# Moving the convolution of a hybrid mixer to VectorE, and reordering the banks, steps and last projections of three mixers

## What is computed

```python
for l in range(2):
    h = rmsnorm(x, norm_mix[l])
    x = x + (even_mixer(h, ...) if l % 2 == 0 else odd_mixer(h, ...))
    x = x + swiglu(rmsnorm(x, norm_ffn[l]), ...)      # d_ff = 2816
```

```python
x = layer_norm(alpha * x + 0.5 * swiglu_2(x, ...))    # d_ff = 4096
x = layer_norm(alpha * x + hybrid_mixer(x, ...))
x = layer_norm(alpha * x + 0.5 * swiglu_2(x, ...))
```

## Time and profile before

| | |
|---|---|
| time, median of 3 runs | 2555.53 us (2553.45 to 2555.55) |
| the profiled execution's own time | 2554.28 us |
| its span, first to last instruction | 2552.2 us |
| PE busy | 2431.1 us, 95% |
| DVE busy | 1801.2 us, 71% |
| ACT busy | 1304.5 us, 51% |
| POOL busy | 115.7 us, 5% |
| mean granted TensorE clock | 0.974 |

### The profile page before, as it was taken

How to read it: one execution, slowest core, us unless ns; L and a number is a source line. 1 busy time by engine, 2 the same in 40 slices (tenths; PEclk the granted TensorE clock), 3 DMA queues, 4 the chain that set the end, 5 groups by cost and what they waited for, 6 DMA issues and landing times.

```text
span 2552.2 us, 39046 instructions
## 1 busy us (share of the span) xinstructions
PE 2431.1 (95%) x15856; PEld 2221.0 (87%) x15856; DVE 1801.2 (71%) x2679; ACT 1304.5 (51%) x1995; POOL 115.7 (5%) x104
## 2 busy tenths in 40 slices
PE   7789999989999999889998999999998899989998
PEld 7678889887888888889998888898888899988887
DVE  4659757567867876777467876688767664678864
ACT  5545454545544544556454554455445663545543
POOL 0002100001200000210000000000002100000000
PEclk9899999999999999999999999999999899999999
DMA  5236565344656565533253656556664332446652
GB/s 182 83 112 213 180 209 181 129 133 144 191 185 198 190 187 185 179 122 108 92 164 126 206 185 187 166 187 198 186 187 160 112 111 97 158 134 204 188 175 91
DMA packets 114882, 409.92 MB, mean 161 GB/s; under 512 B 12816, under 2 KB 14992, under 8 KB 114704
## 3 DMA queue, kind: packets, MB, share of 16 engines
q1 hardware_dynamic: 114704, 407.43, 49.9%
HBM read 406.33 MB, written 1.05 MB: 160 GB/s over the span
## 4 chain that ended last, share of the span: by engine, by line
PE 86%; DVE 9%; ACT 4%; issue 1%; DMA 0%; SPq 0%; ACTq 0%; DVEq 0%
PE ps L359 85%; DVE wlo L1655 3%; ACT whi L1007 1%; ACT region L1170 1%; PE ps L568 0%; DVE x L1812 0%; DVE x L1830 0%; DVE region L1855 0%; DVE xx L1710 0%; DVE region L1950 0%; DMA cst<-in_consts 0%; DVE region L2226 0%; DVE region L2184 0%; DVE region L2312 0%; DVE region L2223 0%
## 5 line engine op out<-in xcount | busy, mean ns | idle before, releaser
L359 PE MATMUL ps<-xx,whi 128*128 128x256 f32 (+1 forms) x4912 | 1346.9, 345 | 40.5 <-ACT region L1404 16.1
L1655 DVE TENSOR_TENSOR wlo<-raw,whi 128x1024 fp32r<-128x1024 f32 (+3 forms) x772 | 935.6, 1217 | 444.5 <-ACT whi L1007 442.9
L1007 ACT ACTIVATE whi<-raw 128x1024 fp32r<-128x1024 f32 (+3 forms) x772 | 800.7, 1043 | 531.4 <-PE ps L359 531.0
L359 PE MATMUL ps<-xx,wlo 128*128 128x256 f32 x3688 | 1046.3, 284 | 0.0
L359 PEld LDWEIGHTS ps<-xx,whi 128*128 128x128 f32 x4912 | 864.8, 193 | 156.5 <-ACT region L1404 16.5
L359 PEld LDWEIGHTS ps<-xx,wlo 128*128 128x128 f32 x3688 | 709.9, 192 | 0.3
L359 PE MATMUL ps<-H,whi 128*128 128x512 f32 (+1 forms) x2400 | 686.7, 351 | 22.1 <-DVE wlo L1655 10.4
L359 PE MATMUL ps<-H,wlo 128*128 128x256 f32 x1888 | 534.7, 283 | 0.0
L359 PEld LDWEIGHTS ps<-H,whi 128*128 128x128 f32 x2400 | 425.5, 191 | 86.4 <-issue 14.6
L359 PEld LDWEIGHTS ps<-H,wlo 128*128 128x128 f32 x1888 | 358.9, 190 | 0.2
L1650 DVE TENSOR_REDUCE t<-ps 128x256 f32<-128x512 f32 x308 | 211.7, 689 | 51.5 <-PE ps L359 42.4
(11 more groups left out here) (271 smaller groups left out, 1564.0 us busy)
## 6 DMA issues: line engine op xcount, KB each, us to landing
raw<-in_sg SPq DMA_DIRECT2D x128, 512.0 KB, 3.8
raw<-in_su SPq DMA_DIRECT2D x128, 512.0 KB, 3.5
raw<-in_sd SPq DMA_DIRECT2D x128, 512.0 KB, 3.9
raw<-in_mw_g SPq DMA_DIRECT2D x48, 512.0 KB, 3.5
raw<-in_fg SPq DMA_DIRECT2D x44, 512.0 KB, 3.4
raw<-in_fu SPq DMA_DIRECT2D x44, 512.0 KB, 3.6
raw<-in_fd SPq DMA_DIRECT2D x32, 512.0 KB, 3.5
raw<-in_mw_a SPq DMA_DIRECT2D x24, 512.0 KB, 3.8
```

Source lines behind the costliest of these rows:

```text
L359: return e.matmul(out, lhsT, rhs, start=start, stop=stop, skip_group_check=True)
L1007: e.activation(m.whi[:, c % NHL, 0:cw], m.raw[:, c % NRAW, 0:cw], ACT.Copy).then_inc(s["whi"].h, s["whi"].up(c))
L1655: e.tensor_tensor(m.wlo[:, c % NHL, 0:cw], m.raw[:, c % NRAW, 0:cw], m.whi[:, c % NHL, 0:cw].bitcast(F32), ALU.subtract).then_inc(s["wlo"] ...
```

## The change

**Projections end two tiles at a time.** The last four chunks of `ew_out` and `ow_out` are laid out anew, so that one chunk holds the last 512 input rows for two output tiles. `gemm_last` runs them: after each chunk one bank is finished. Each of its chunks needs all four of the last input tiles.

**Banks of the feed-forward networks after a rmsnorm.** `first_bank` makes them start at bank 4; the statistics go to bank 3. One weight chunk more is made ahead of the statistics (`produce(1)`).

**even().** Two chunks of `ew_v` come ahead of `ukv`. `k_pe` is made transposed (16 matmuls of 512 and 256 columns), summed by one reduce and transposed back by two transposes; VectorE sums the squares so that four one-column matmuls are left of 20. Two chunks, not four, are made ready before x is split, and ScalarE's first table load is taken by a dummy instruction at the start. One gelu of 128 x 1024 replaces four of 128 x 256. The side steps in the first four `ew_out` chunks are two to a chunk.

**odd().** Heads start at chunks 0, 7 and 14 of `ow_g` and at chunk 4 of `ow_out`, with more empty steps inside; `side.finish()` stands once, ahead of `gemm_last`.

**hybrid().** All convolution taps but the first are made by VectorE; GpSimd keeps the copies of the identity. `mw_c` uses banks 0 to 3, its scaled bias is computed first, two of the six `raw` go behind it, the wait for `rowc` moves back. `attend` has a further empty step in places, `delta()` starts one chunk later. In `mw_o` tiles 0 to 7 use banks 2, 3, 4, 5, 0, 1, 6, 7, the centring uses bank 1, and one `chunk()` moves ahead of `norm_tile(2)`.

```diff
@@ weight_order()
-    o = [("ew_c", i) for i in range(5)] + [("ew_pe", 0)]
+    o = [("ew_c", i) for i in range(5)] + [("ew_pe", 0), ("ew_v", 0), ("ew_v", 1)]
...
+def first_bank(kind, j):
+
+    return 2 * ((j + (2 if kind == "rms" else 0)) % 4)
...
+    m.mo_bank = [2, 3, 4, 5, 0, 1, 6, 7]
@@ tensor_program
+    def gemm_last(name, i, tag, hb):
+
+        for p in range(4):
+            wh, wl = weights(name, i + p)
+            for n in range(2):
+                o = ps[p][:, n * 256:n * 256 + 256]
+                for k in range(4):
+                    w.wait_ge(s["hlo"], *tag(k))
+                    c = (n * 4 + k) * 128
+                    t = mm3(o, wh[:, c:c + 128], wl[:, c:c + 128], hb[0][:, k, :], hb[1][:, k, :], False, k == 3)
+            t.then_inc(s["gemm"].h, s["gemm"].up(name, i + p))
@@ ffn
-            return take(2 * (j % 4) + g, ("fsum", st, j, g))
+            return take(first_bank(kind, j) + g, ("fsum", st, j, g))
...
-            rms_stats(st)
+            rms_stats(st, bank=3)
@@ even, TensorE
-        gemm_tm("ew_pe", 0, [take(5, ("edve", "kpe"))], xh, xl, 8, 8, 32)
-        b = take(6, ("root", "rr", 1))
+        wh, wl = weights("ew_pe", 0)
+        b = take(5, ("edve", "kpf"))
+        for k in range(8):
+            c = slice(k * 32, k * 32 + 32)
+            mm(b[0:32, :], wh[:, c], m.xx[:, k].rearrange("p a b -> p (a b)"), start=k == 0, stop=False)
+            t = mm(b[0:32, 0:256], wl[:, c], xh[:, k, :], start=False, stop=True)
...
+        value(0)
+        w.wait_ge(s["edve"], "kpf")
...
+        value(1)
...
         for k in range(4):
             w.wait_ge(s["hlo"], "ea", k)
-            gemm_acc("ew_out", k, h1[0], h1[1], k, k == 0, False, readers)
-            side.step()
-        for k in range(4):
-            side.until(lambda: k in ot)
-            w.wait_ge(s["hlo"], "eo", k)
-            gemm_acc("ew_out", 4 + k, h2[0], h2[1], k, False, k == 3, readers)
+            gemm_acc("ew_out", k, h1[0], h1[1], k, k == 0, readers, side.step)
             side.step()
         side.finish()
+        gemm_last("ew_out", 4, lambda k: ("eo", k), h2)
@@ odd, TensorE
         for i in range(16):
             gemm_fm("ow_g", i, take(i % 4, ("rdve", "g", i))[:, 0:256], xh, xl)
-            if i in (6, 12):
-                side.add(head(0 if i == 6 else 1))
+            if i in (0, 7, 14):
+                side.add(head(i // 7))
+            side.step()
+        readers = [[("xadd", "f1", p)] for p in range(4)]
+        for c in range(12):
+            h, k = c // 4, c % 4
+            w.wait_ge(s["hlo"], "o", c)
+            gemm_acc("ow_out", c, hb[h % 2][0], hb[h % 2][1], k, c == 0, readers)
+            if c == 4:
+                side.add(head(3))
             side.step()
         side.finish()
...
+        gemm_last("ow_out", 12, lambda k: ("o", 12 + k), h2)
@@ even, ScalarE
-            w.wait_ge(s["edve"], "u", i)
-            e.activation(m.euF[:, i, :], m.euF[:, i, :], ACT.Gelu_apprx_tanh).then_inc(s["eact"].h, s["eact"].up("u", i))
...
+            if i == 3:
+                w.wait_ge(s["edve"], "u", 3)
+                e.activation(m.euF[:, :, :], m.euF[:, :, :], ACT.Gelu_apprx_tanh).then_inc(s["eact"].h, s["eact"].up("u"))
@@ hybrid, VectorE
         def conv(i):
+
             y, pr = m.cv[:, i, :], m.pr[i]
-            w.wait_ge(s["cpool"], l, i)
...
+            w.wait_ge(s["pact"], l, "a3", i)
+            for d in (1, 2, 3):
+                e.scalar_tensor_tensor(y[:, d:256], pr[:, 0:256 - d], pk(f"cw{l}", 12 * (3 - d) + i), y[:, d:256], ALU.mult,
+                                       ALU.add).then_inc(s["cdve"].h, s["cdve"].up(l, d, i))
+                w.wait_ge(s["cdve"], l, d, i)
+
...
         for n in range(8):
-            norm_tile(f"t{l}", (f"l2g{l}", f"l2b{l}"), n, 3, add_one, (f"mw_o{l}", n), n)
-            if n >= 3:
+            if n == 2:
+                chunk()
+            norm_tile(f"t{l}", (f"l2g{l}", f"l2b{l}"), n, 3, add_one, (f"mw_o{l}", n), m.mo_bank[n])
+            if 3 <= n < 7:
                 chunk()
@@ hybrid, GpSimd
-        for i in range(12):
-            pr, y, r = m.pr[i], m.cv[:, i, :], m.tap[i % 2]
-            w.wait_ge(s["pact"], l, "a", i)
-            if i >= 2:
-                w.wait_ge(s["cpool"], l, i - 2)
-            e.tensor_scalar(r, pr, pk(f"cw{l}", 24 + i), None, ALU.mult).then_inc(s["cpool"].h, s["cpool"].up(l, "r", i))
-            w.wait_ge(s["cpool"], l, "r", i)
-            w.wait_ge(s["pact"], l, "a3", i)
-            e.tensor_tensor(y[:, 1:256], y[:, 1:256], r[:, 0:255], ALU.add).then_inc(s["cpool"].h, s["cpool"].up(l, i))
-        w.wait_ge(s["cpool"], l, 11)
+        w.wait_ge(s["gemm"], f"mw_a{l}", 7)
```

More of the change, by code:

```diff
@@ L428, in gemm_tm, with gemm_acc @@
                 after()
-    def gemm_acc(name, i, ah, al, k, first, last, readers):
+    def gemm_acc(name, i, ah, al, k, first, readers, half=None):
         wh, wl = weights(name, i)
@@ L448, in rms_stats @@
             w.wait_ge(s["xsq"], st, 7)
[L449 removed]
+        b = take(bank, ("root", st))
         mm(b[:, 0:256], m.onm, acc[0], start=True, stop=False)
@@ L559, in attend @@
                     yield
-            for _ in range(gap):
+            for _ in range(gaps[h0 // 4]):
                 yield
@@ L645, in even @@
         side.add(heads(1))
-        gemm_tm("ew_v", 0, [take(2 + tt, ("eact", "v", tt)) for tt in range(2)], xh, xl, 8, 2, 512, after=side.step)
+        for c in (2, 3):
+            value(c)
+            side.step()
         for i in range(4):
@@ L1189, in even @@
         rms_parts("e", "nm0", ("in",))
-        chunk(4)
-        chunk(0)
+        chunk(2)
+        chunk()
         rms_stats("e", RT=True)
+        for _ in range(2):
+            chunk()
         for i in range(5):
-            if i == 4:
-                chunk()
             dst = m.cq[:, i, :] if i < 3 else m.ckv[:, i - 3, :]
@@ L1303, in even @@
             side.step()
-        for k in range(4):
-            side.until(lambda: k in ot)
-            chunk()
             side.step()
         side.finish()
+        for _ in range(4):
+            chunk()
     def odd():
@@ L1356, in odd @@
             e.activation(m.sg[:, i, :], m.sg[:, i, :], ACT.Silu).then_inc(s["ract"].h, s["ract"].up("g", i))
-            if i in (6, 12):
-                side.add(head(0 if i == 6 else 1))
+            if i in (0, 7, 14):
+                side.add(head(i // 7))
+            side.step()
+        for c in range(12):
+            chunk()
+            if c == 4:
+                side.add(head(3))
             side.step()
         side.finish()
-        for h in range(4):
-            if h < 3 and h + 1 not in ot:
-                side.add(head(h + 1))
-            for k in range(4):
-                if k == 0 and h not in ot:
-                    side.finish()
-                chunk()
-                side.step()
-            side.finish()
+        for _ in range(4):
+            chunk()
     def hybrid(l):
@@ L1395, in hybrid @@
             tap(i)
-        for i in range(6, 8):
+        for i in range(4):
+            produce(1, 4)
+            raw(i)
+        for _ in range(2):
             chunk()
-            taps(i)
         for i in range(5):
@@ L1454, in hybrid @@
             taps(i)
-            if i == 11:
-                for p in range(5):
-                    conv(p)
             side.step()
@@ L1543, in hybrid @@
                 s["pact"].h, s["pact"].up(l, "qk", i))
-            if i == 1:
-                conv(5)
+            if i == 2:
+                for p in range(6):
+                    conv(p)
                 side.add(delta())
@@ L1598, in hybrid @@
                 w.wait_ge(s["xlo"], f"g{l}", 7)
-            norm_tile(f"t{l}", (f"l2g{l}", f"l2b{l}"), n, 3, 0)
+            norm_tile(f"t{l}", (f"l2g{l}", f"l2b{l}"), n, 3, 1)
     w.wait_ge(s["set"], "onm")
-    for _ in range(4):
+    e.activation(m.junk0, m.epsc[:, 0:1], ACT.Copy)
+    for _ in range(2):
         upper(done[1])
@@ L2014, in even @@
                 s["hlo"].h, s["hlo"].up("e", i))
+        for _ in range(2):
+            chunk()
+        w.wait_ge(s["eps"], "kpe")
+        w.wait_ge(s["rstd"], "e", "T")
+        e.tensor_tensor(m.kpe, ps[5][:, 0:64].rearrange("p (a b) -> p a b", b=32),
+                        m.eRT.unsqueeze(2).broadcast_to([128, 2, 32]), ALU.mult).then_inc(
+            s["edve"].h, s["edve"].up("kpe"))
         w.wait_ge(s["root"], "rr", 1)
@@ L2686, in lay_out @@
     d["ow_g"] = fm(w[:, 4096:6144])
-    d["ow_out"] = a["odd_w_out"][0].reshape(16, 128, 1024)
+    d["ow_out"] = out(a["odd_w_out"][0])
     for i in range(2):
```

283 lines of the change are left out of this document (159 added, 124 removed).

## The result

The changed kernel takes 2528.25 us (median of 4 runs, 2526.29 to 2528.6) against 2555.54 beside it. The ratio is 0.9889, with a 95% interval of 0.9871 to 0.9907: faster, by 27 us or 1.1%, clear of the noise. The forecast was 2492, a gain of 63.4, so less than half of it came. The time lies in the range, near its upper end.

What follows compares the result with a forecast made beforehand. TensorE was taken as the bound: its work, idle time and low clock. Gains of 19.3 + 17.8 + 9.1 + 8 + 9.2 = 63.4 us took 2555.5 to 2492 us, range 2456 to 2533.

Steps and rivals of the forecast that it cites:

- D: Front of both hybrid mixers: four mw_c banks remove the 8.06 us wait, 4 us a layer, 8 gained; bounds −12 to 37.
- The rest of the wait comes again as one of 3 to 4 us ahead of the first scores: Hybrid front: tile 4 comes only some 4 us earlier, so part of the 8.06 us wait returns before the window scores.
- The count of the taps at nothing: Hybrid front: 12 taps a layer moved to VectorE cost 5.8 us, offset by less GpSimd contention; net counted as zero.
- 12 such chunks give 6.4 back: Hybrid front: without GpSimd's contention a wlo takes 1.23 instead of 1.76 us, returning 6.4 us over 12 chunks.
- B: Inside the odd mixer: each wait gets more cover than it lacks, 13.7 idle plus 5.1 clock less 1.0: 17.8 us gained.
- C: Inside the even mixer: attention's chain sets the end; earlier chain and two links a chunk gain 9.1 us, bounds −4 to 25.
- slower: Rival, chance 0.05: half chunks are too little cover in ew_out and the odd mixer, 118 us lost against 63 won, 2610.
- A: Starts of the two rmsnorm networks: the 6.72 us wait falls to about 1.2; 9.7 us each, 19.3 gained for two.
- E: mw_o of the hybrid layers: waits of 1.57 and 5.20 us shrink or go; 4.6 a layer, 9.2 us gained.
- Less: Rival, chance 0.20: side steps and gemm_last turn into waits of their own; 23.4 us gained, 2532.
- the estimate from the Trainium skill's 2.66 us a switch: Even mixer's table loads: counting a drain, four removed loads free 10.6 us of ScalarE, not 5.1; gain there some 14.
- The forecast's rule of nothing lost behind waits under 2 us: TensorE clock: about 4 us at half clock, 1.9 lost, behind each wait of 2 us or more, nothing behind shorter ones.

Runs made afterwards that it cites:

- the kernel with the old body: The changed kernel with the whole hybrid mixer body as before (taps on GpSimd, two mw_c banks, steps, delta rule start), new mw_o kept: 2510.85 us, ratio 0.9827.

## Why the prediction was wrong

**D is where it failed.** It said 8 won and 15.3 were lost. "The rest of the wait comes again as one of 3 to 4 us ahead of the first scores" was right (4.10). What it took the four banks to be worth, 4 us a layer, was not: the two kernels that differ in the banks, the early bias and the wait for `rowc` have 663.6 and 662.6 in both layers together, 1.0 and not 8. And the sum of D held no term for the edits that move the side chains: the added steps of `attend`, the start of `delta()` a chunk later, the taps and silus gathered ahead of it. They stand in the change and none was priced. Taken off the changed kernel one after the other they are 8.0 (start), 3.6 (raw tiles), 8.2 (places of taps and silus); 682.4 then becomes 662.6. With the 3.6 won from the old body (666.3) to this 662.6, they give −16 where the table has −15.3. That they do so is no second check, since they are the steps of one row of kernels; what the runs show is the size of each. They don't add up in every order: the late start costs 8.0 beside the new places and 13.1 without, and the steps save 19.2 beside the late start and cost 7.4 without it on the new front. Of the 9.0 us that the first body lost, 2.3 are idle time (16.0 to 18.3 from its first matmul to `mw_o`), and the clock of windows of 12 us over it gives some 5 more (11.9 lost before, 16.9 now); 1.7 stay unassigned. What of the steps' effect is the meeting with the decay chain and what the place of the squares is not settled.

The count of the taps at nothing was right (666.4 us with GpSimd's tap and 666.3 without it on the old body), but not for the reason given. The term "12 such chunks give 6.4 back" is not in the trace: of the 24 full `wlo` in the 120 us from the first hybrid matmul of the kernel before, five took 1.57 to 1.77 us and the others 1.21 to 1.23. Between the two kernels with the old body, VectorE's instructions in such a stretch add up to 91.9 us with GpSimd's tap and to 90.9 without. The 12 taps added 5.7; `wlo` gave 3.0 back, the small instructions of 8 columns 2.2, the other two taps 0.9.

**B was mis-sized.** It said that each wait "has more cover than it lacks". The 5.9 us of the norm's waits became 1.77, the rest as said; but the step forgot that `ow_out` begins in the banks that hold the last gate tiles, whose reads on VectorE come late: 3.3 us, of which the kernel with bank 4 took 2.6 away. Whether the gating of head 1 makes them late is open, since with the heads at 0, 6 and 12 a read was late without it, behind a `wlo` that waited 3.7 us for ScalarE. The waits ahead of `gemm_last` were 1.8 and not 1.0. Saved are 13.7 − 7.3 = 6.4 of idle time and 3 to 4 of clock, 9.7 together in these two profiles and 7 to 10 over all kernels with this code, where the step had 17.8.

**C came out right by its number, 9.7 for 9.1, with most links in place**: first matmul at 14.08 for 14.1, the last split piece 0.42 behind 131.53 for 131.6, `gemm_last` ending at 142.5 for 143.1.

```profile
126.12 0.42 DVE L1726 TENSOR_TENSOR H<-ps,H 128x256 fp32r<-128x256 f32 x1 [2.61 <-ACT H L1283]
129.13 0.42 DVE L1726 TENSOR_TENSOR H<-ps,H 128x256 fp32r<-128x256 f32 x1
131.53 0.42 DVE L1726 TENSOR_TENSOR H<-ps,H 128x256 fp32r<-128x256 f32 x1 [1.98 <-ACT H L1283]
```

What it drew from them was wrong, so the number is in part luck. It took the denser steps as the source of the gain: from the maxima of heads 4 to 7 (ending at 112.7, for 112.9) to the last split piece there were 29.2 us before and 19.3 now, for 18.7. But with one step to a chunk it takes 15.1, and the network starts some 5 us earlier. So the denser steps gave 5 away, and what shortened the 29.2 no run took apart. The idle time of the stretch did not fall either, it rose from 20.6 to 22.9, with the 10.23 at 72.67; the gain is in TensorE's busy time, 115.5 to 105.6 us, with 42 matmuls fewer and the clock at 0.91 for 0.87. The rival *slower* had this mechanism, half a chunk as too little cover, at the right place and far too wide.

**A and E were right.** The first matmul of the first network stands 1.51 behind the projection, for 1.2, with the clock at 1.00 behind it (144 to 152 us); undone, the banks cost 14 us. The fifth chunk took its wait from 1.51 to 1.01 and not to nothing, 0.5 of the 1.5 for each. The waits of 1.57 and 5.20 are gone in E, with 1.01 and 1.91 new behind them; it gave 9.2 in the timelines and 9.9 by the kernel with the old body, the latter good to some 4.

**The rivals.** *Less* named a size near the result, 2532, but through C, B and E, with D at 0; the loss came from D. On the table loads: C came to 9.7, not to some 14, the estimate from the Trainium skill's 2.66 us a switch ("ScalarE: Activation LUTs", What ACT_TABLE_LOAD costs). That decides nothing, since C's steps were not all right, and no run isolates a table load. The trace of the kernel before agrees with the 1.283 us of the load and shows no drain as idle time: the load at 108.71 stands 0.02 us behind the activation before it, and the next starts 0.01 us behind the load. The prediction's "at once behind it" holds there only; behind the other five loads of the softmax region the next activation came 0.3 to 2.2 us later, having waited for VectorE.

**4.1 us are no effect of the change**: the code of that stretch is the same, and the pace of its matmuls differs from one execution to another, as the last section shows.

## What to carry to other kernels

An edit that only moves links of a side chain has a price like any other: follow the chain to its end, and ask at each link what matmuls now lie beside it, before counting it at nothing. A wait that is removed ahead of a chain pays only if the chain's first operand is earlier too; here a wait of 7.1 us came back as two, of 5.0. When a change bundles several moves, price the pairs: here the new front and the new steps, harmless alone, cost 8 us together, and undoing the steps alone, beside the late delta rule, lost 19. And take the spread of the same code from all executions at hand before reading a few microseconds out of two timelines.

## What the runs showed of the hardware that was not expected

The same matmuls run at two speeds while the clock reads 1.00. In the wide layer ahead of the hybrid ones a pair of matmuls starts every 347 ns in some executions and every 353 in others, with the same code and no idle time (ten and eight of the 18 profiled executions). The windows of the kernel before and of the changed kernel in that layer:

```profile
824.00:844.00 20.00, 20.00 (x118) 17.62 (x117) 16.57 (x23) 10.34 (x15) 0.00 (x0) 1.00 0.56 184
```

```profile
788.00:808.00 20.00, 20.00 (x115) 17.32 (x114) 16.06 (x22) 10.02 (x14) 0.00 (x0) 1.00 0.58 193
```

From the first matmul of the second rmsnorm network to the first hybrid layer, where most kernels have the same code, it took 473.0 to 479.6 us in 16 profiled executions; the changed kernel's own, 479.6, was among the longest. In the layers from the first hybrid one on, the pair took 353 or 354 ns in each of them. What sets it is open.

The clock behind short waits is not settled by their length. Ahead of and inside `gemm_last` of the odd mixer, waits of 1.07 to 1.08 and 0.77 to 0.79 us left it at 1.00 in seven of 17 executions and were followed by 0.50 in ten, where the rest of the 96 matmuls took 12.1 us instead of 10.2 to 10.6. What decides it is open. The forecast's rule of nothing lost behind waits under 2 us was too kind.
